# Two feed-forward down projections as seven block products instead of eight, with the sums of weight blocks formed in DRAM

## What is computed

```python
h = rmsnorm(x, norm_ffn[i])
x = x + (jax.nn.silu(h @ w_gate[i]) * (h @ w_up[i])) @ w_down[i]   # (512x2816) @ (2816x1024)
```

## Time and profile before

| | before |
|---|---|
| time, median of 3 runs | 1580.95 us (1580.85 to 1581.01) |
| profiled execution: own time | 1581.13 us |
| profiled execution: span, first to last instruction | 1579.3 us |
| TensorE busy | 1571.0 us of the span |
| VectorE, ScalarE, GpSimd busy | 1067.9, 723.0, 130.5 us |
| DMA | 164.07 MB, mean 104 GB/s |
| granted TensorE clock | 0.999 |

### The profile page before, as it was taken

How to read it: one execution, slowest core, us unless ns; L and a number is a source line. 1 busy time by engine, 2 the same in 40 slices (tenths; PEclk the granted TensorE clock), 3 DMA queues, 4 the chain that set the end, 5 groups by cost and what they waited for, 6 DMA issues and landing times.

```text
span 1579.3 us, 23274 instructions
## 1 busy us (share of the span) xinstructions
PE 1571.0 (99%) x8492; PEld 1309.2 (83%) x8492; DVE 1067.9 (68%) x1583; ACT 723.0 (46%) x1270; POOL 130.5 (8%) x121
## 2 busy tenths in 40 slices
PE   9999999999999999999999999999999999999998
PEld 7877888999988876778899988887777778888887
DVE  7666678888833366767888885438667657556566
ACT  6333345666722345554566663322455542233334
POOL 2000200000010100030000001114111111000000
PEclk9999999999999999999999999999999999999999
DMA  6422333333323341133333355343121121333344
GB/s 226 147 80 81 101 99 106 103 106 104 126 92 102 68 109 47 39 102 107 104 100 105 105 182 211 127 177 119 54 68 54 41 61 41 87 106 93 95 128 152
DMA packets 48941, 164.07 MB, mean 104 GB/s; under 512 B 6011, under 2 KB 9308, under 8 KB 48476
## 3 DMA queue, kind: packets, MB, share of 16 engines
q1 hardware_dynamic: 44752, 152.46, 31.2%
q10 hardware_dynamic: 4108, 10.52, 2.0%
HBM read 156.38 MB, written 6.59 MB: 103 GB/s over the span
## 4 chain that ended last, share of the span: by engine, by line
PE 97%; DVE 2%; issue 0%; ACT 0%; POOL 0%; DVEq 0%; POOLq 0%; ACTq 0%
PE ps L2497 21%; PE ps L2499 20%; PE ps L2498 20%; PE ps L2720 5%; PE ps L2719 5%; PE ps L2718 5%; PE ps L2726 4%; PE ps L2728 2%; PE ps L3036 1%; PE ps L3058 1%; PE ps L3024 1%; PE ps L2833 1%; PE ps L2866 1%; PE ps L3164 1%; PE ps L3163 1%; PE ps L3162 1%
## 5 line engine op out<-in xcount | busy, mean ns | idle before, releaser
L1478 DVE TENSOR_TENSOR w_lo<-raw,w_hi 128x1024 fp32r<-128x1024 f32 (+4 forms) x184 | 242.6, 1318 | 129.1 <-ACT w_hi L853 128.4
L853 ACT ACTIVATE w_hi<-raw 128x1024 fp32r<-128x1024 f32 (+4 forms) x184 | 193.6, 1052 | 295.2 <-PE ps L2499 269.6
L2497 PE MATMUL ps<-a_hi,w_hi 128*128 128x512 f32 x632 | 255.6, 404 | 0.7 <-DVE t L1513 0.4
L2499 PE MATMUL ps<-a_hi,w_lo 128*128 128x512 f32 x632 | 246.8, 391 | 0.0
L2498 PE MATMUL ps<-a_lo,w_hi 128*128 128x512 f32 x632 | 246.4, 390 | 0.0
L2497 PEld LDWEIGHTS ps<-a_hi,w_hi 128*128 128x128 f32 x632 | 118.7, 188 | 32.5 <-issue 7.8
L2499 PEld LDWEIGHTS ps<-a_hi,w_lo 128*128 128x128 f32 x632 | 118.6, 188 | 25.9
L2498 PEld LDWEIGHTS ps<-a_lo,w_hi 128*128 128x128 f32 x632 | 118.9, 188 | 22.0
L2497 PE MATMUL ps<-g_hi_b,w_hi 128*128 128x512 f32 x246 | 95.7, 389 | 0.0
L2498 PE MATMUL ps<-g_lo_b,w_hi 128*128 128x512 f32 x246 | 95.7, 389 | 0.0
L2499 PE MATMUL ps<-g_hi_b,w_lo 128*128 128x512 f32 x246 | 95.7, 389 | 0.0
(11 more groups left out here) (463 smaller groups left out, 3737.8 us busy)
## 6 DMA issues: line engine op xcount, KB each, us to landing
raw<-w SPq DMA_DIRECT2D x134, 512.0 KB, 3.6
raw<-w8b SPq DMA_DIRECT2D x62, 512.0 KB, 3.6
raw<-w_down SPq DMA_DIRECT2D x32, 704.0 KB, 4.1
w<-cmp_w SPq DMA_DIRECT2D x2, 2048.0 KB, 11.2
raw<-block_spill SPq DMA_DIRECT2D x8, 512.0 KB, 4.7
raw<-w_blocks SPq DMA_DIRECT2D x6, 512.0 KB, 4.4
raw<-w_out_first SPq DMA_DIRECT2D x8, 320.0 KB, 2.8
even_row<-w_last ACTq DMA_DIRECT2D x4, 512.0 KB, 5.4
```

The source lines that it names most:

```text
L853: act.activation(w_hi[:, slot, 0:w], raw[:, raw_slot, 0:w], ACT.Copy)\
L1478: dve.tensor_tensor(w_lo[:, slot, 0:w], raw[:, raw_slot, 0:w], w_hi[:, slot, 0:w].bitcast(F32), ALU.subtract).then_inc(w_lo_ready, 1)
L2497: pe.matmul(o, wh, a_h, start=start and at == 0, stop=False)
L2499: ins = pe.matmul(o, wl, a_h, start=False, stop=stop and at == kt - 1)
```

## The change

**The down projection.** The k dimension (22 tiles) is cut in two halves of 11, the tokens in two of 256, the features in two of 512. Seven products of 256 tokens by 512 features by 11 k-tiles replace eight (`DOWN_ORDER`): three use blocks of `w_down` as they are (b11, b21, b22), four use sums of blocks (t1 to t4). The stationary operand is now a g tile (128 tokens), the moving one 512 columns of weights, so results are token-major. 44 strips of 11 blocks in ones and twos replace 16 (`DOWN_STRIPS`), in four slots of split weights (`down_slot`). ScalarE copies PSUM between products, VectorE forms two sums in PSUM, and 32 transposes (`turned`) bring each layer's result back to feature-major. The first two strips of the next stage are multiplied together, tile by tile (`two_strips`), with the last 8 transposes among them (`rest`).

**Mixtures of activations.** GpSimd forms the four sums of g blocks (`mixtures`), two instructions each.

**Sums of weight blocks.** GpSimd issues DRAM to DRAM transfers (`add_blocks`): for each set four copies and four accumulating transfers, each waited for before the next. There is one set of 2816 KB transfers per layer, and after that of layer 1 one of 1024 KB transfers for `w_out_2`, which replaces the 16 sums on VectorE and their loads and stores.

**Around it.** Sums of squares, the spread and some loads and waits behind each down projection move by up to a strip; some semaphores are merged. Signs in the last product change with the new sums.

The core of the diff:

```diff
+FIRST_K = list(range(PLAIN, PLAIN + HALF))
+SECOND_K = list(range(PLAIN + HALF, FT)) + list(range(PLAIN))
+DOWN_ORDER = ["b11", "t3", "t2", "b21", "t1", "t4", "b22"]
+DOWN_TILES = [[2, 2, 2, 2, 1, 1, 1]] + [[2, 2, 2, 2, 2, 1]] * 5 + [[2, 2, 2, 2, 1, 1, 1]]
+DOWN_STRIPS = [(i, sum(tiles[:s]), c) for i, tiles in enumerate(DOWN_TILES) for s, c in enumerate(tiles)]
+DOWN_FIRST = [sum(map(len, DOWN_TILES[:i])) for i in range(len(DOWN_TILES) + 1)]
+DOWN = len(DOWN_STRIPS)
+EARLY = 6
...
+            def load_down(layer, n0):
+                for s, (i, q, c) in enumerate(DOWN_STRIPS):
+                    kind = DOWN_ORDER[i]
+                    if kind == "t3" and q == 0:
+                        sp.wait_ge(sums_in, 16 * 8 * (layer + 1))
+                    block = a["w_down"][layer, BLOCKS.index(kind)] if kind in BLOCKS else \
+                        down_sums[layer, SUMMED.index(kind)]
+                    rows = bass.AP(tensor=block.tensor, offset=block.offset + q * P * S,
+                                   ap=[[S, P], [P * S, c], [1, S]])
+                    sp.wait_ge(w_lo_ready, n0 + s - (RAW - 1))
+                    sp.dma_start(raw[:, s % RAW, 0:c * S].rearrange("p (c s) -> p c s", c=c), rows)\
+                        .then_inc(raw_in[s % RAW], 16)
+
+            load_down(0, N_DOWN0)
...
-                if n == N_SECOND + RAW:
+                if n == N_SECOND + RAW + 1:
                     sp.wait_ge(lin_read, out_index(N_SECOND))
+                    sp.wait_ge(acc2_ready, 1 + KT)
...
+            def add_blocks(blocks, sums, before):
+                (b11, b12, b21, b22), (t1, t3, t2, t4) = blocks_and_sums(blocks, sums)
+                for i, (dst, src) in enumerate(((t1, b12), (t3, b12), (t2, b22), (t4, b21))):
+                    pool.dma_start(dst, src).then_inc(sums_in, 16)
+                    pool.wait_ge(sums_in, 16 * (before + i + 1))
+                for i, (dst, src) in enumerate(((t3, b22), (t1, b11), (t2, t1), (t4, t2))):
+                    pool.dma_start(dst, src, accum_op=ALU.add, max_dma_last_dim=8192).then_inc(sums_in, 16)
+                    pool.wait_ge(sums_in, 16 * (before + i + 5))
+
+            def mixtures(layer, n0, q0):
+
+                def subtracted(dst, first, second, what):
+                    for lot in range(2):
+                        pool.tensor_tensor(dst(LOTS[lot]), first(LOTS[lot]), second(LOTS[lot]), ALU.subtract)\
+                            .then_inc(mix_ready, 1)
+                    pool.wait_ge(mix_ready, mixes(layer, what + "+"))
+
+                def a11(lot):
+                    return g_lot(0, lot, 0)
+
+                def a21(lot):
+                    return g_lot(0, lot, 1)
+
+                def a12(lot):
+                    return g_lot(1, lot, 0)
+
+                def a22(lot):
+                    return g_lot(1, lot, 1)
+
+                pool.wait_ge(blk_done, n0)
+                pool.wait_ge(lin_read, q0 - 10)
+                subtracted(lambda lot: odd_sum[:, lot[0]:lot[1], :], a11, a21, "s3")
+                pool.wait_ge(lin_read, q0)
+                subtracted(a21, a21, a22, "s1")
+                pool.wait_ge(g_lo_ready, made(layer, 0, 0))
+                subtracted(a11, a11, a21, "s2")
+                pool.wait_ge(g_lo_ready, made(layer, 3, 2))
+                subtracted(a12, a12, a11, "s4")
...
+            add_blocks(a["w_down"][1], down_sums[1], 8)
+            add_blocks(a["w_blocks"], out_sums, 16)
+            mixtures(1, N_DOWN1, out_index(N_DOWN1))
...
+                def weights(s):
+                    hi = down_slot(s)[0]
+                    act.wait_ge(raw_in[s % RAW], 16 * ((n0 + s) // RAW + 1))
+                    if s < 4:
+                        act.wait_ge(blk_done, n0)
+                        if s == 3:
+                            act.wait_ge(lin_read, q0)
+                    elif s == DOWN - 3:
+                        act.wait_ge(down_sum, 3 * layer + 2)
+                    elif s < DOWN - 3 or s == DOWN - 1:
+                        act.wait_ge(blk_done, n0 + s - 3)
+                    act.activation(hi, raw[:, s % RAW, 0:hi.shape[1]], ACT.Copy).then_inc(w_hi_ready, 1)
...
+                for s in range(DOWN):
+                    i = DOWN_STRIPS[s][0]
+                    at = s - DOWN_FIRST[i]
+                    if at == 0:
+                        if i == 1:
+                            copied(ps[:, 0:2, :], ps[:, 4:6, :], 1, down_copy, scale=-1.0)
+                        if i == 2:
+                            copied(held_down[:], ps[:, 2:4, :], 2, down_copy)
+                        if i == 3:
+                            copied(ps[:, 6:8, :], ps[:, 0:2, :], 3, down_copy)
+                        if i == 4:
+                            copied(c11[:], ps[:, 4:6, :], 4, down_out)
+                        if i == 6:
+                            copied(c21[:], ps[:, 0:2, :], 6, down_out)
+                    if s and s + 3 < DOWN:
+                        weights(s + 3)
+                    if at in ((1, 2) if i else (2, 4)) and i + 1 < len(DOWN_ORDER):
+                        rounded(i + 1, int(at > (1 if i else 2)))
+                    if i == 5 and at == 4:
+                        copied(c22[:], ps[:, 2:4, :], 5, down_out, 2)
+                    if i == 6:
+                        if at in (4, 5, 6):
+                            following(n0 + DOWN + at - 4)
+                        if 2 <= at < 6:
+                            residual(at - 2, q0 + at - 2, v, g, at % 2, first=at < 4)
+                act.wait_ge(blk_done, n0 + DOWN)
+                act.activation(c12[:, 0, :], ps[:, 6, :], ACT.Copy).then_inc(down_out, 1)
+                for m in range(4, KT):
+                    residual(m, q0 + m, v, g, m % 2)
...
+                def added(m):
+                    dve.wait_ge(down_turn, KT * layer + m + 1)
+                    dve.tensor_tensor(x[:, m, :], x[:, m, :], ps[:, DOWN_TURNS[m], :], ALU.add).then_inc(lin_read, 1)
+
...
+                    if i == 3 and at == 1:
+                        dve.wait_ge(down_copy, 3 * layer + 3)
+                        dve.tensor_tensor(ps[:, 0:2, :], held_down[:], ps[:, 0:2, :], ALU.subtract).then_inc(down_sum, 1)
+                    if i == 5 and at == 0:
+                        dve.wait_ge(blk_done, n0 + DOWN_FIRST[5])
+                        dve.tensor_tensor(ps[:, 2:4, :], ps[:, 6:8, :], held_down[:], ALU.subtract).then_inc(down_sum, 1)
+                    if at in ((1, 2) if i else (2, 4)) and i + 1 < len(DOWN_ORDER):
+                        left(i + 1, int(at > (1 if i else 2)))
+                    if i == 6:
+                        if at in (1, 2):
+                            added(2 * at - 2)
+                            added(2 * at - 1)
+                        if 2 <= at < 6:
+                            operand(at - 2, g, count + at - 1)
+                        if at in (4, 5, 6):
+                            following(n0 + DOWN + at - 4)
+                dve.wait_ge(blk_done, n0 + DOWN)
+                dve.tensor_copy(c12[:, 1, :], ps[:, 7, :]).then_inc(down_sum, 1)
+                added(4)
+                added(5)
+                for m in range(4, KT):
                     operand(m, g, count + m + 1)
-                    split(n + 3, KT * P if m == KT - 1 else SLOT, 1, (2 * j + 3) % 4)
-                    if m in (0, 2):
-                        row_sums(1 if m == 0 else 2)
+                    if m + 2 < KT:
+                        added(m + 2)
...
+
+                def turned(m, blocks):
+                    bank = DOWN_TURNS[m]
+                    for b, c in blocks:
+                        ins = pe.transpose(ps[:, bank, b * P:(b + 1) * P], c[:, b % 2, m % 4 * P:(m % 4 + 1) * P],
+                                           ident[:])
+                    return ins
+
+                for s, (i, q0_, c) in enumerate(DOWN_STRIPS):
+                    n, kind, at = n0 + s, DOWN_ORDER[i], s - DOWN_FIRST[i]
+                    bank = DOWN_BANK[kind]
+                    if at == 0:
+                        if kind == "b11":
+                            pe.wait_ge(lin_read, q0 - 3)
+                        if kind == "t3":
+                            pe.wait_ge(lin_read, q0)
+                        if kind == "t2":
+                            pe.wait_ge(down_copy, 3 * layer + 1)
+                        if kind == "t1":
+                            pe.wait_ge(down_copy, 3 * layer + 3)
+                        if kind == "t4":
+                            pe.wait_ge(down_sum, 3 * layer + 1)
+                        if kind == "b22":
+                            pe.wait_ge(down_sum, 3 * layer + 2)
+                    pe.wait_ge(w_lo_ready, n + 1)
+                    wh, wl = down_slot(s)
+                    for j in range(c):
+                        q = q0_ + j
+                        if i == 0:
+                            pe.wait_ge(g_lo_ready, MADE * layer + q + 1 if q < EARLY else made(layer, 0, 0))
```

(52 more changed lines are left out.)

478 lines of the change are left out of this document (239 added, 239 removed).

## The result

The changed kernel takes 1598.83 us (median of 4 runs, 1598.13 to 1600.26) against 1580.98 us before: ratio 1.0113, 95% interval 1.010 to 1.0127. That is 17.9 us slower where 17.4 us faster was forecast. The profiled execution has a span of 1595.9 us at a mean granted clock of 0.992 (before 1579.3 us).

A forecast was written before the change was run, and what follows sets the result against it. TensorE, busy in every slice, was taken as the bound. Terms of -29.9 + 7.0 + 0.6 + 4.5 + 0.4 = -17.4 us took 1581.13 to 1563.7 us, median 1563.5; range 1556 to 1598 us.

The forecast's parts named there:

- GpSimd's mixtures: Down projection: each mixture takes GpSimd 7.4 to 11.7 us, ready in time; no cost, at worst 2 us per layer.
- The start of a down projection: First strips' weight splits on ScalarE and VectorE nearly keep up; 0.3 us of waiting per layer, 0.6 us in all.
- Inside it: Within each 15.0 us product of a down projection, ScalarE's 9.8 us and VectorE's 10.1 to 11.4 us fit; no cost.
- the end: Behind each down projection, TensorE waits for splits, the block's copy and GpSimd's additions; 4.5 us for both layers together.
- 0.4 for others: Strip loads queued behind the first `cmp_w` load, which waits for GpSimd's last addition, and all such places: 0.4 us.
- Rival 3: The down projection stage's ends cost more, with slow GpSimd additions and mixtures: 1570 to 1575 us; chance 0.12.
- the two large terms: TensorE in both down projections: 132 fewer matmuls save 29.9 us, 64 added transposes cost 7.0 us.
- the sums in DRAM: Transfers beside TensorE's work, done before the down projection needs them: copies 9.5 to 15.4 us, accumulating 17 to 31; no wait.
- Rival 1: Layer 1's sums in DRAM come late, stopping all engines: slower, 1620 us at 40 us per large accumulating transfer; chance 0.16.
- rival 2: Transfers forming sums starve the feed-forward's own loads, 0 to 29 us per layer: 1575 to 1595 us; chance 0.10.
- The forecast's own test: Whole kernel: the forecast counts as wrong if TensorE idles over 12 us in all.

The follow-up runs named there:

- run 1: The changed kernel with GpSimd's eight mixtures per layer replaced by memsets of 4 columns, so the sums of activations are left out: 1573.05 us.
- run 7: The changed kernel with GpSimd's mixtures cut into pieces of one k-tile (256 columns) in place of 1280 and 1536 columns: 1602.52 us.
- run 4: The kernel before, with GpSimd subtractions, memsets and copies of 512 columns added in layer 0's down projection, nine at a time: 1586.51 us.
- runs 9 to 11: Block's copy first at the ends: with VectorE making the mixtures, 1573.71 us; changed kernel, mixtures on GpSimd, 1601.35; changed kernel without mixtures, 1573.78.
- run 8: The kernel before, TensorE held up at down projection starts, once by about 5.6 us in layer 0, twice by about 2.9 in layer 1: 1595.95 us.
- run 3: The changed kernel without the 24 transfers that form sums in DRAM, loading block b12 where a sum would be loaded: 1597.76 us.

## Why the prediction was wrong

**The step that failed** is *GpSimd's mixtures*: "I take no cost, and 2 us per layer as the other end". It measured 13.4 us per layer (run 1). The price of a mixture was right (7.4 to 8.1 us in a range of 7.4 to 11.7), and no run shows a fault in its due times. Wrong was to ask only when a mixture ends, and not what it does to the engine beside it. *The start of a down projection* (0.3 us per layer) and *Inside it* rested on durations from the earlier trace rows, which are VectorE's beside a silent GpSimd. The means of those rows hide it, since GpSimd was busy 8% of the span before. The kernel before does show it in single rows, which the prediction didn't read: this is its VectorE timeline behind layer 1's down projection. At 1054.43 GpSimd adds squares, and the 1024 columns take 2.16 us.

```profile
1054.43 2.16 DVE L1478 TENSOR_TENSOR w_lo<-raw,w_hi 128x1024 fp32r<-128x1024 f32 x1 [1.33 <-ACT w_hi L853]
...
1073.91 1.00 DVE L2102 TENSOR_TENSOR windows<-vcr,pe 64x496 f32<-64x496 f32 x1
...
1084.20 1.92 DVE L2102 TENSOR_TENSOR windows<-vcr,pe 64x496 f32<-64x496 f32 x1
```

The last of these rows runs beside the very GpSimd row of 2.13 us (1083.18) that the prediction took from the earlier trace rows as "where GpSimd was slow": the same `windows` sum takes VectorE 1.92 us there and 1.00 without GpSimd. The slow rate was a sign of the two engines holding each other up.

The Trainium skill, SBUF — State Buffer, "Who interferes with whom", has this rule: a VectorE instruction with two inputs in SBUF contends with a GpSimd instruction that reads SBUF, and not with one that only writes; the one that starts first blocks the other for its whole length. One with a single SBUF input, outside VectorE's two-port modes, doesn't contend. The runs agree on subtractions (1.30 us against 0.61), on memsets and on the operand in PSUM (both unslowed), and run 7 and the 1.45 us of run 4 agree on whole instructions of GpSimd's. They don't show the delay for GpSimd's copies, which read SBUF, nor for every instruction beside its subtractions (1.68 us at 484.34 in run 4, 1.26 at 426.25 in run 7), and GpSimd was held up in run 7 but not in run 4.

**The second failed term** is the end: 4.5 us for both layers and 0.4 for others. From the next stage's first matmul the changed kernel needs 5.8 us more than before up to the `e_sw` copy and 8.3 us in layer 1, 14.1 in all, of which 1.8 are transposes: 12.3 us, 7.4 more than forecast. Part of it is the same slowing, as GpSimd adds squares there. VectorE's splits for the next stage, priced at 1.2 us, take 2.3 us each in the changed kernel's layer 1:

```profile
1056.31 2.31 DVE L2033 TENSOR_TENSOR w_lo<-raw,w_hi 128x1024 fp32r<-128x1024 f32 x1
...
1060.25 2.28 DVE L2033 TENSOR_TENSOR w_lo<-raw,w_hi 128x1024 fp32r<-128x1024 f32 x1
1062.45 2.30 DVE L2033 TENSOR_TENSOR far_lo<-raw,far_hi 128x1024 fp32r<-128x1024 f32 x1
```

TensorE waits 2.8 us there for the second `w_lo`, a wait that the sum doesn't have, then 1.9 us for the copy (2.8 forecast), and runs at the lower clock until 1070.6 us. Another part is a chain that the sum priced too low: the norm's sum, root and spread. All eight tiles of the residual now come within 26 us (VectorE's additions to x start from 1045.1 to 1070.1 us in layer 1), where one came every 15 us before, and the chain follows them with little work left to cover it. It costs the changed kernel a wait of 1.2 us in layer 0, and 4.7 us once the waits ahead of it are gone (runs 9 to 11). *Rival 3* named this place, and its range, 1570 to 1575 us, was still too low.

**The clock** was in no term. Together with the restarts it makes each wait cost more than its length: 13.4 us per layer stand for 9.4 and 8.0 us of waits. That the gaps by themselves bring it is shown by run 8.

**Right** were the two large terms: 132 matmuls and 64 transposes give 107.4 us per down projection, measured without mixtures 107.75. Right was that *the sums in DRAM* are hidden. GpSimd's timeline in the changed kernel, where the idle time in brackets is that of the transfer before:

```profile
217.81 0.53 POOL L851 DMA_DIRECT2D down_sums<-w_down  x1 [11.69 <-DMA down_sums<-w_down]
...
318.96 0.94 POOL L854 DMA_DIRECT2D down_sums<-down_sums  x1 [18.56 <-DMA down_sums<-down_sums]
```

The other idle times of this kind are 11.3 to 13.8 us behind copies of 2816 KB and 18.3 to 19.9 behind accumulating ones; with the issue itself (0.5 to 1.0 us) a copy takes 12 to 14 us, inside my 9.5 to 15.4, and an accumulating transfer 19 to 21, inside 17 to 31. In layer 1 the last one was issued at 906.73, 31 us before the down projection's first matmul. *Rival 1* didn't happen, and neither did *rival 2*: the loads of `w` land after 5.1 us (median) in place of 3.6, and without the transfers the time is only 1.1 us shorter (run 3).

**The account**, for both layers: forecast 1563.5; mixtures 2 x 13.4 = 26.8, on top of the forecast's start, which run 1 has as well (107.75 against 107.4); ends 7.4. That gives 1597.7 us, against 1598.1 for the profiled execution, which these terms are read from, and a median of 1598.8. The forecast's own test, that it is wrong if TensorE idles over 12 us, was met: it waited 25 us in the down projections and behind them (17.4 + 7.7).
